# Attention projections: each group's values first, their turns spread between the banks of queries and keys

## What is computed

```python
h = rms_norm(x, g_mix)                     # (1024, 1024)
proj = h @ w_in                            # columns: [pool 256 | q 768 | k 768 | v 768]
for gi, (window, dilation) in enumerate(((128, 1), (512, 4), (2048, 16))):
    # 4 heads of 64 per group: banded attention over each residue class mod dilation
    o, lse = dilated_window_attention(q_g, k_g, v_g, window, dilation, slopes_g)
alpha = softmax(lse over the three groups)
x = x + concat(pool_out, alpha * o) @ w_out
```

## Time and profile before

| what | value |
|---|---|
| median of 3 runs | 2577.65 us |
| the profiled execution's own time | 2577.02 us |
| its span (first to last instruction) | 2575.0 us |
| mean granted TensorE clock | 0.993 |
| TensorE matmul busy | 2513.7 us (98%) |
| attention's projections and units on TensorE | 47.65 to 350.6 us |

### The profile page before, as it was taken

The page is one execution under the profiler, slowest core; times in us unless marked ns, Lnnn a source line. Parts: engine busy times, 40 slices in busy tenths (PEclk is TensorE's granted clock), DMA queues, the critical chain, the costliest instruction groups (busy, mean ns, idle before and its releaser), DMA issues.

```text
span 2575.0 us, 41533 instructions
## 1 busy us (share of the span) xinstructions
PE 2513.7 (98%) x15177; PEld 2247.5 (87%) x15177; DVE 2116.4 (82%) x4504; ACT 879.8 (34%) x1658; POOL 1509.7 (59%) x1046
## 2 busy tenths in 40 slices
PE   8999989999999999998999999998999999999998
PEld 6777768999999999998999999987888888888887
DVE  7022273699999999999999997789998999989998
ACT  4223252322222222234777773232222222222222
POOL 2111030346777778886666668856665676666663
PEclk9999999999999999998999999999999999999999
DMA  4110022337899999998999999999999999999995
GB/s 155 49 33 25 26 89 99 123 111 233 308 337 335 351 330 357 347 341 304 395 398 394 400 401 410 400 380 377 381 375 380 367 379 379 376 379 369 377 374 212
DMA packets 296672, 763.35 MB, mean 296 GB/s; under 512 B 25824, under 2 KB 116320, under 8 KB 293728
## 3 DMA queue, kind: packets, MB, share of 16 engines
q0 software_dynamic: 110592, 402.70, 41.7%
q1 hardware_dynamic: 161280, 288.81, 31.9%
q10 hardware_dynamic: 24672, 70.33, 7.1%
HBM read 669.47 MB, written 92.27 MB: 296 GB/s over the span
## 4 chain that ended last, share of the span: by engine, by line
PE 66%; DVE 12%; POOL 4%; DMA 3%; issue 1%; ACT 1%; SPq 0%; another core or an unknown queue 0%; DVEq 0%; ACTq 0%
PE bank L1793 25%; PE bank L2199 19%; PE wide L2199 13%; DVE u_row L1469 5%; PE bank L2167 3%; PE bank L2020 3%; PE bank L2077 2%; POOL w_lo L718 2%; POOL u_row L735 2%; DMA g_first<-g_d 1%; DVE rest_k L1436 1%; DVE ix L1439 1%; POOL u_row L730 1%; DVE ix L1442 1%; DMA u_row<-in_u_rows,ids 1%
## 5 line engine op out<-in xcount | busy, mean ns | idle before, releaser
L786 POOL DMA_INDIRECT d_row<-in_v,ids x330 | 564.2, 1710 | 297.0 <-DVE yg L1691 225.2
L1793 PE MATMUL bank<-h_hi,w_hi 128*128 128x320 f32 (+1 forms) x2368 | 557.1, 316 | 8.6 <-POOL w_lo L718 7.9
L1793 PE MATMUL bank<-h_hi,w_lo 128*128 128x320 f32 (+1 forms) x2368 | 546.5, 312 | 0.0
L1793 PE MATMUL bank<-h_lo,w_hi 128*128 128x320 f32 (+1 forms) x2368 | 546.3, 312 | 0.1
L718 POOL TENSOR_TENSOR w_lo<-w_raw,w_hi 128x512 fp32r<-128x512 f32 (+1 forms) x230 | 367.1, 1614 | 178.3 <-DVE gate_j L1611 95.4
L730 POOL DMA_INDIRECT u_row<-in_u_rows,ids x384 | 403.7, 1051 | 110.9 <-issue 82.2
L1469 DVE CUSTOM_DVE_ANT_0 u_row<-wide,u_row 128x1024 f32<-128x1024 f32 x384 | 449.6, 1220 | 10.3 <-DMA u_row<-in_u_rows,ids 6.2
L1691 DVE SCALAR_TENSOR_TENSOR yg<-d_row,uh,yg 128x1024 f32<-128x1024 f32 x330 | 409.8, 1277 | 1.5
L1793 PEld LDWEIGHTS bank<-h_hi,w_hi 128*128 128x128 f32 x2368 | 395.4, 189 | 14.4 <-POOL w_lo L718 7.5
L1793 PEld LDWEIGHTS bank<-h_lo,w_hi 128*128 128x128 f32 x2368 | 399.2, 189 | 2.9 <-issue 0.4
L1793 PEld LDWEIGHTS bank<-h_hi,w_lo 128*128 128x128 f32 x2368 | 398.7, 189 | 2.5
(11 more groups left out here) (234 smaller groups left out, 4131.1 us busy)
## 6 DMA issues: line engine op xcount, KB each, us to landing
w_raw<-in_u SPq DMA_DIRECT2D x128, 512.0 KB
v_raw<-in_v ACTq DMA_DIRECT2D x126, 512.0 KB
act_d<-act_st SPq DMA_DIRECT2D x128, 320.0 KB
g_d<-g_st SPq DMA_DIRECT2D x20, 2048.0 KB
a_raw<-act_d SPq DMA_DIRECT2D x154, 256.0 KB
g_raw<-g_d SPq DMA_DIRECT2D x120, 256.0 KB
w_raw<-in_w_q SPq DMA_DIRECT2D x32, 512.0 KB
w_raw<-in_w_in SPq DMA_DIRECT2D x20, 512.0 KB
```

What stands on the lines that cost most here:

```text
L786: nc.gpsimd.indirect_dma_start(d_row[k % DR][:, :], None, v_rows, bass.IndirectOffsetOnAxis(ids[:, c:c + 1], 0)).then_inc(d_in[k % DR], 16)
L1793: ins = pe.matmul(banks[h][:, 0:n], lhs[:, part], rhs[:, k, h * n:(h + 1) * n], start=(k == 0 and lhs is lhs_hi and rhs is h_hi), stop=(k ...
```

## The change

Each group's pieces are used in the order v0, v1, q0, q1, k0, k1. All steps of a group stand in one list, `STEPS[g]`: 8 half-steps of v, then for each of the 8 banks of q and k its two half-steps and behind them one or two turned tiles. TensorE and ScalarE both follow that list. `steps_by` shares it by cost (a half-step 8, a turned tile 1) over 15 units in place of 12, and rounds up to whole steps. In group 0 the pooling product stands behind step 17 (three q and k banks and three tiles), and `project` (two banks at once) is gone. The lead of group 1 now stands ahead of the wait for `PJ_G[0]` and of `qk(0, 0)`. `PIECE_BANKS` is counted anew in this order; the upper halves of q0 and q1 are made behind the take of the last v bank.

```diff
-        HALVES, BUSY_UNITS = 24, 12
+        V_FIRST = (4, 5, 0, 1, 2, 3)
+        STEPS = []
         for g in range(GROUPS):
+            tiles = len(turned_tiles(g))
+            steps = [("v", m, half) for m in range(4) for half in range(2)]
             banks += 4
             PIECE_BANKS += [banks] * 2
             PJ_VT.append(banks)
+            for m in range(8):
+                steps += [("p", m, half) for half in range(2)]
+                banks += 1
+                if m % 2:
+                    PIECE_BANKS.append(banks)
+                turned = range(tiles * m // 8, tiles * (m + 1) // 8)
+                steps += [("t", j, 1) for j in turned]
+                banks += len(turned)
+            STEPS.append(steps)
             PJ_G.append(banks)
+        BUSY_UNITS, LEAD, POOL_AT = 15, 2, 17
         def steps_by(g, k):
+            lead, cost = LEAD if g == 1 else 0, [1 if kind == "t" else 8 for kind, _, _ in STEPS[g]]
+            upto = sum(cost[:lead]) + (sum(cost[lead:]) * min(k + 1, BUSY_UNITS) + BUSY_UNITS - 1) // BUSY_UNITS
+            return next(n for n in range(lead, len(cost) + 1) if sum(cost[:n]) >= upto)
...
+                    if kind == "v":
+                        dst = v_turned(g, m % 2).rearrange("p (r l) -> p r l", r=n_res)
+                        take(...)
+                        if m == 3:
+                            for n in (4 + 6 * g, 5 + 6 * g):
+                                upper_slot(n, n)
+                    elif kind == "p":
+                        q, hf, n = m // 2, m % 2, 4 + 6 * g + m // 2
+                        take(...)
+                        if hf and n + 2 < IN_PIECES:
                             upper_slot(n + 2, n + 2)
+                    else:
+                        rows = turned_tiles(g)[m][1]
+                        take(vt[g % 2][0:rows, m, :], lambda b: b[0:rows, 0:4 * DH])
...
-            for k in range(4):
-                project(2 + k)
+            projection_steps(0, 0, POOL_AT)
...
-            projection_steps(0, 16, HALVES + len(turned_tiles(0)))
+            projection_steps(0, POOL_AT, len(STEPS[0]))
             pe.wait_ge(pool_ev, 4)
...
+            projection_steps(1, 0, LEAD)
             pe.wait_ge(pj_free, PJ_G[0])
             qk(0, 0)
             asked = 1
-            projection_steps(1, 0, steps_by(1, -1))
```

More of the change, by code:

```diff
@@ L461, in build @@
         PIECE_BANKS, PJ_VT, PJ_G, banks = [3, 4], [], [], 4
+        V_FIRST = (4, 5, 0, 1, 2, 3)
+        STEPS = []
         for g in range(GROUPS):
-            for _ in range(4):
-                banks += 2
-                PIECE_BANKS.append(banks)
+            tiles = len(turned_tiles(g))
+            steps = [("v", m, half) for m in range(4) for half in range(2)]
             banks += 4
@@ L468, in build @@
             PJ_VT.append(banks)
-            banks += len(turned_tiles(g))
+            for m in range(8):
[7 more added lines that the diff above has]
+            STEPS.append(steps)
             PJ_G.append(banks)
@@ L474, in build @@
         PJ_ALL = PIECE_BANKS[-1]
-        HALVES, BUSY_UNITS = 24, 12
+        BUSY_UNITS, LEAD, POOL_AT = 15, 2, 17
         def steps_by(g, k):
[L481 to L484, removed]
+            lead, cost = LEAD if g == 1 else 0, [1 if kind == "t" else 8 for kind, _, _ in STEPS[g]]
+            upto = sum(cost[:lead]) + (sum(cost[lead:]) * min(k + 1, BUSY_UNITS) + BUSY_UNITS - 1) // BUSY_UNITS
+            return next(n for n in range(lead, len(cost) + 1) if sum(cost[:n]) >= upto)
         def parts_by(g, k):
-            steps = steps_by(g, k)
-            return min(steps, HALVES) // 2 + max(steps - HALVES, 0)
+            return sum(half for _, _, half in STEPS[g][:steps_by(g, k)])
         def v_turned(g, c):
@@ L573, in _ @@
             for n in range(2, IN_PIECES):
-                load_piece(n, win_d[n])
+                load_piece(n, win_d[2 + (n - 2) // 6 * 6 + V_FIRST[(n - 2) % 6]])
                 if n == 2:
@@ L905, in projections @@
                     act.wait_ge(pv_done, UNITS)
[L906 to L909, removed]
+                for kind, m, half in STEPS[g]:
+                    if not half:
+                        continue
+                    if kind == "v":
+                        dst = v_turned(g, m % 2).rearrange("p (r l) -> p r l", r=n_res)
+                        take(dst[:, :, m // 2 * length // 2:(m // 2 + 1) * length // 2],
+                             lambda b: b[:, :].rearrange("p (l r) -> p r l", r=n_res))
+                        if m == 3:
[3 more added lines that the diff above has]
+                        q, hf, n = m // 2, m % 2, 4 + 6 * g + m // 2
+                        dst = (qt if q < 2 else kt)[g % 2][:, q % 2, :].rearrange("p (r l) -> p r l", r=n_res)
                         take(dst[:, :, hf * length // 2:(hf + 1) * length // 2],
@@ L912, in projections @@
                              -DH ** -0.5 if q < 2 else 1.0)
-                        if hf:
+                        if hf and n + 2 < IN_PIECES:
                             upper_slot(n + 2, n + 2)
[L915 to L926, removed]
+                    else:
+                        rows = turned_tiles(g)[m][1]
+                        take(vt[g % 2][0:rows, m, :], lambda b: b[0:rows, 0:4 * DH])
                     yield
@@ L936, in _ @@
                     if k or g == 1:
-                        for _ in range(parts_by(g, k - 1) - (parts_by(g, k - 2) if k > (g != 1) else 0)):
+                        for _ in range(parts_by(g, k - 1) - (parts_by(g, k - 2) if k else 0)):
                             next(work, None)
@@ L1842, in _ @@
             pj = [4]
[L1844 to L1851, removed]
             def project_half(n, h, half):
@@ L1869, in project_v @@
             def project_v(g, m, half):
-                n, c, hf = 6 + 6 * g, m % 2, m // 2
+                n, c, hf = 2 + 6 * g, m % 2, m // 2
                 b = pj[0]
@@ L1900, in projection_steps @@
             def projection_steps(g, s0, s1):
[L1902 to L1907, removed]
+                for kind, m, half in STEPS[g][s0:s1]:
+                    if kind == "t":
+                        turn_v(g, m)
+                    elif kind == "p":
+                        project_half(4 + 6 * g + m // 2, m % 2, half)
                     else:
-                        project_v(g, m - 8, half)
+                        project_v(g, m, half)
             def qk(g, k):
@@ L2002, in _ @@
                 if g + 1 < GROUPS:
-                    projection_steps(g + 1, steps_by(g + 1, k - 1) if k or g == 0 else 0, steps_by(g + 1, k))
+                    projection_steps(g + 1, steps_by(g + 1, k - 1), steps_by(g + 1, k))
                 m = n - (GROUPS - 1) * UNITS - 2
```

## The result

The changed kernel takes 2596.55 us (median of 5, 2594.99 to 2604.71), the kernel before beside it 2578.16 us (5 runs, 2576.46 to 2582.03): ratio 1.0076, 95% interval 1.0055 to 1.0097, so slower by 19.6 us (14.2 to 25.0). The forecast was 2596.6 us. Timed once more later, six runs beside eleven of before, the same kernel gave 1.0098 (1.0080 to 1.0116), 25.2 us. The profiled execution of after spans 2593.0 us, 18.0 more than before's. TensorE's busy time, from the page's first part, grew by 8.1 us against the earlier trace rows with the same 15177 instructions; the rest is idle time.

What follows compares the result with a forecast made beforehand. TensorE, 98% busy, was taken as the bound. Stage losses of 6.5, 4.2 and 4.1 us (+14.8) plus 4.2 for the clock made +19.0, giving 2596.6 us, range 2588 to 2602.

Steps and rivals of the forecast that it cites:

- the wait between values and queries: Between last v and first q half-step, once per group: TensorE waits for the slot hand-over, 4.25 us, three times.
- Rivals 3 and 4: 3: values-to-queries wait hidden, +2.1 us, chance 0.06; 4: that and new group-end waits absent, -5.8 us, chance 0.03.
- Group ends: Added waits in group 0's v1, the lead, ahead of unit 0 and in each group's last unit, 0.9 to 4.2 us each.
- v1 of group 0: Second v half-step of group 0: waits for POOL's lower half of piece 3, 1.95 us.
- The lead: Group 1's first steps, ahead of unit 0: the second half-step waits for v1's slot, 0.9 us.
- Scores bare: Behind `qk(0, 0)`, ahead of unit 0: exponentials no longer lie under the lead, 2.36 us.
- Last unit of group 0: Unit 15, without steps: next `qk` waits for takes and an upper half, then exponentials, 4.2 us.
- Last unit of group 1: Last unit before unit 32, without steps: `qk` waits for one tile's take, then exponentials, 2.9 us.
- A turned tile by itself: Single tiles between projections: 0.22 us plus 0.10 for the restart, 0.32 us each; 29 tiles 9.3 us, bounds 6.4 to 14.5.
- The clock: Behind each of the three values-to-queries waits: TensorE's clock falls, 1.4 us each, 4.2 us; bounds nothing and twice that.
- Rival 2: Clock also falls at shorter waits (group 0's v1, ahead of unit 0, unit 15), six falls: +14.8 + 8.4, 2600.9 us; chance 0.12.
- forecast 14.8: Attention stage's net loss without the clock: group 0 +6.5, group 1's steps +4.2, group 2's steps +4.1 us.

Runs made afterwards that it cites:

- e1: Changed kernel with all four first value half-steps ahead of the four second ones, so slots free earlier; ratio 1.0004 to the kernel before, +1.0 us.
- e5: Changed kernel with qk(0, 0) and the wait for the last takes put ahead of group 1's lead; ratio 1.0086 to the kernel before, +22.2 us.
- e2: Changed kernel with 16 unread matmuls ahead of each group's first query half-step, filling the wait; ratio 1.0038 to the kernel before, +9.8 us.
- e6: e1 plus e5's edit, with turned tiles spread over the first seven query and key banks; ratio 0.9962 to the kernel before, -9.8 us.
- e10: Changed kernel run again, unedited; ratio 1.0098 to the kernel before, +25.2 us.
- e3: Changed kernel with one step moved in groups 1 and 2, so a unit's fixed part stands between values and queries; ratio 1.0061 to before, +15.8 us.
- e7: Kernel before with 108 unread matmuls ahead of group 0's first query piece, otherwise unchanged; ratio 1.0113 to the kernel before, +29.2 us.
- e8: Kernel before with 54 unread matmuls ahead of group 0's first query piece, otherwise unchanged; ratio 1.0063 to the kernel before, +16.3 us.

## Why the prediction came out, step by step

- **The deciding step, "the wait between values and queries", held.** Three times, in group 0, unit 3 and unit 20, released by POOL. Start to start it is 75.79 - 71.35 - 0.23 = 4.21 us against 4.25 (the rows gave 121.25 - 117.12 = 4.13, which I read as 4.2). Rivals 3 and 4 needed it to be absent; e1 shows what they would have seen.
- **Group ends held.** v1 of group 0: 1.75 against 1.95. The lead: 0.88 against 0.9. Scores bare: 136.72 - 134.25 = 2.47 against 2.36. Last unit of group 0: 239.73 - 235.49 = 4.24 against 4.2. Last unit of group 1: 2.97 (345.79 to 348.76) against 2.9.
- **"A turned tile by itself" was too dear.** In the timeline below a tile's two transposes stand between two projections; the last two rows are the first matmuls behind the next two tiles:

```profile
104.05 0.39 PE L1858 MATMUL bank<-h_hi,w_lo 128*128 128x512 f32 x1
104.28 0.38 PE L1891 MATMUL bank<-ident,ot 128*128 128x128 f32 x2
104.42 0.48 PE L1858 MATMUL bank<-h_hi,w_hi 128*128 128x512 f32 x1
104.73 0.39 PE L1858 MATMUL bank<-h_lo,w_hi 128*128 128x512 f32 x1
...
110.11 0.48 PE L1858 MATMUL bank<-h_hi,w_hi 128*128 128x512 f32 x1
...
115.81 0.48 PE L1858 MATMUL bank<-h_hi,w_hi 128*128 128x512 f32 x1
```

  104.28 - 104.05 is one pace, and to 104.73 go 0.45 us for the tile and one more pace: 0.22 for the tile, the lower bound. From tile to tile, over a whole bank, it is a little more: 5.69 and 5.70 us less 24 x 0.227 = 5.44 leave 0.25. So the restart is 0.03 us and not 0.10, and if these two stand for all 29, 29 x 0.07 = 2.0 us of the sum did not exist.
- **"The clock" was mis-sized, and this is the step that failed.** I took 1.4 us, from twelve matmuls of which only part ran slow, at three places: 4.2. A fall behind a bare wait of 4.05 us costs 1.75, 2.56 and, in unit 20, 2.57 (278.48 to 283.77, less 2.72), as the lower level's pace is 0.43 us a matmul against 0.23. And it fell at two more: unit 0 takes 8.36 us (136.72 to 145.08) against 6.75 in e5, where that unit is at full pace, and unit 16 10.46 (239.73 to 250.19) against before's 7.44. In all 1.75 + 2.56 + 2.57 + 1.6 + 3.0 = 11.5 us. I had also leaned on a wrong row: "the 1.72 us wait at 120 us brought no fall (1.00)" names the window that ends at 120 us, before the wait is over. The one behind it has 1.00 as well:

```profile
120.00:130.00 10.00, 9.13 (x48) 6.81 (x49) 0.91 (x5) 5.08 (x15) 3.61 (x2) 1.00 0.33 105
```

  Rival 2 had the right places in part (ahead of unit 0 and in unit 15, not the v1 wait) at too low a price.
- **So the stage was under-forecast and the time was not.** 24.5 - 11.5 = 13.0 us stand beside the forecast 14.8, and the 2.0 of the tiles account for the difference but for 0.2; the clock adds 7.3. At unit 32 the kernel is 24.5 us late against 19.0; rival 2's stage, 14.8 + 8.4 = 23.2, was nearer. That the median of five is 2596.55 and not some 2601 lies within what five runs can tell (14.2 to 25.0, the second timing 20.6 to 29.9). The direction and mechanism were right; the agreement to 0.1 us is luck, and 20 to 25 us is the better figure for the change.

The Trainium skill ("TensorE: Matmul & The Clock Gate", section "HAM oscillation — how this bites in real kernels") says that a few microseconds without matmuls between two bursts let the engine begin the second at half rate. The trace agrees at all three waits, 0.43 us a matmul against 0.23. The example there has some 1.67 us at half rate for each gap; here the slow part lasts 3.5 us once (75.79 to 79.31) and 5.3 us twice, and the measurement decides. In units 0 and 16 the clock fell behind shorter waits as well, of 0.88 and 1.88 us and of 1.29 and 1.18 us.

What stays open: the part beyond the stage in e2 (stage +18.0, timed +9.8, 3.9 to 15.5) and e6 (stage -3.8, timed -9.8, -13.9 to -5.7). No run here separates a real effect behind the stage from the spread of runs.

## What to carry to other kernels

When steps are moved, look for the place where the order runs into a slot that is freed late: between the last use of a buffer and the first use of what refills it lies the whole hand-over through the other engines (here 4.2 us), and what stood there before was its cover, however idle it looked. Freeing the buffer earlier (e1) took away all of the loss; evening out the work was worth 2 to 4 us. Price a bare wait of TensorE with the slow matmuls behind it, by the slow pace that a row shows times their number, and not by a mean over a stretch that was only partly slow; and give that price a range, here 1.5 to 2.9 us behind the same wait of 4.05 us.

## What was not expected of the hardware

How long the granted clock stays low behind the same wait differs, and whether it falls behind a short one depends on more than the wait.

Behind the bare wait of 4.05 us in group 0 the 24 matmuls of the first q bank take 7.21 us in after, 8.31 in e10, which is the same kernel, 8.24 in e3 and 6.98 in e5; 24 paces are 5.44.

For a short wait the nearest pair is e1 and after at unit 16. The instructions and the waits ahead of it are the same to 0.01 us, and e1's unit takes 7.44 us (223.15 to 230.59), after's 10.46; the first transposes show 0.63 us here and 1.06 in after's row at 239.73 above.

```profile
220.79 0.59 PE L1917 MATMUL bank<-kt,qt 64*128 64x192 f32 x4 [1.29 <-ACT vt L877]
...
223.15 0.63 PE L1931 MATMUL wide<-ident,pr 128*64 128x128 f32 x4 [1.18 <-ACT pr L899]
```

In before, TensorE waits 1.72 and 0.75 us at the end of group 0 and the window from 120 us has 1.00 (above). In e7 the same code, moved back by some 25 us, has nearly the same waits (1.71 and 0.56 us), and the clock falls: ten transposes take 2.29 us in place of 1.48, four score matmuls 1.01 in place of 0.60, and the window's granted clock is 0.88.

```profile
144.90 2.29 PE L1895 MATMUL bank<-ident,ot 128*128 128x128 f32 x10 [1.71 <-ACT vt L872]
...
147.75 1.01 PE L1922 MATMUL bank<-kt,qt 64*128 64x192 f32 x4 [0.56 <-ACT vt L872]
```

```profile
130.00:150.00 20.00, 17.70 (x79) 13.91 (x78) 0.65 (x4) 8.24 (x17) 4.67 (x2) 0.88 0.11 29
```

That costs some 2.5 us at unit 0, which is 27.3 us late for 108 matmuls that take 24.5 at full pace. In e8 it falls too (0.85 in the window from 135 to 145 us). And e3 has one fall and one escape behind nearly equal waits. So a wait of one to two and a half microseconds may or may not cost a fall. Shifting the code in time is enough to bring one (e7, e8), and even two executions of the changed kernel differ: unit 0 takes 8.36 us in one and 6.77 in the other. That is part of why unit 32 differs by 1.2 us between the two, and of why e6's unit 16, behind waits of 0.25 and 1.18 us, still takes 8.99 us against 7.44 before. What decides it, no run here shows.
